# A gated delta rule in chunks of 128 tokens instead of 64, in a fused attention and MLP block on one Trainium2 core

## The reference

```python
h = rms_norm(x, pre_mix_norm)
proj = h @ w_in                     # q, k, v, gates of both mixers
fox_o = forgetting_attention(...)   # 8 heads x 64, causal, softmax
# gated delta rule, 4 heads x 128, chunk = C tokens
decay = exp(gc[:, None] - gc[None, :])          # lower triangle
m     = strict_lower((k * beta) @ k.T) * decay
t_inv = inverse(I + m)
u, w  = t_inv @ (v * beta), t_inv @ (k * beta * exp(gc))
a     = (q @ k.T) * decay
for each chunk:
    v_new = u - w @ state
    o     = (q * exp(gc)) @ state + a @ v_new
    state = state * exp(gc[-1]) + (k * exp(gc[-1] - gc)).T @ v_new
x = x + rms_norm(concat(fox_o, gdn_o) @ w_out)
x = x + rms_norm(relu(rms_norm(x) @ w_up) ** 2 @ w_down)
```

## Time and profile before

| | |
|---|---|
| median of three runs | 1646.76 us (1643.49 to 1648.24) |
| the profiled execution's own time | 1642.12 us |
| its span in the profile | 1640.1 us |
| PE busy | 1534.6 us, 94% |
| DVE, ACT, POOL busy | 56%, 40%, 36% |

### The profile page before, as it was taken

How to read it: one execution, slowest core, us unless ns; L and a number is a source line. 1 busy time by engine, 2 the same in 40 slices (tenths; PEclk the granted TensorE clock), 3 DMA queues, 4 the chain that set the end, 5 groups by cost and what they waited for, 6 DMA issues and landing times.

```text
span 1640.1 us, 22146 instructions
## 1 busy us (share of the span) xinstructions
PE 1534.6 (94%) x7769; PEld 1231.6 (75%) x7769; DVE 924.5 (56%) x1538; ACT 652.0 (40%) x1371; POOL 585.0 (36%) x496
## 2 busy tenths in 40 slices
PE   4999999999999999998987998999999999899997
PEld 3877876787777877787765886788787786688885
DVE  5355256542565335645342459776676659944557
ACT  4343245522445234453441435233332343345444
POOL 1005133341324322252330026666665429831001
PEclk7999999999999999999677998999999999999999
DMA  5111001200102011011104333444444696333533
GB/s 186 39 58 34 14 21 32 66 26 14 52 7 59 27 27 39 14 52 52 40 1 165 117 103 96 142 141 148 143 152 143 215 375 209 85 97 98 196 97 140
DMA packets 135043, 152.75 MB, mean 93 GB/s; under 512 B 9436, under 2 KB 89612, under 8 KB 134936
## 3 DMA queue, kind: packets, MB, share of 16 engines
q1 hardware_dynamic: 134936, 151.32, 28.6%
HBM read 109.31 MB, written 41.99 MB: 92 GB/s over the span
## 4 chain that ended last, share of the span: by engine, by line
PE 67%; DVE 13%; POOL 6%; issue 6%; DMA 5%; ACT 2%; SPq 0%; DVEq 0%; POOLq 0%; ACTq 0%
PE ps L2085 7%; PE ps L2028 6%; PE ps L2029 6%; PE ps L2030 6%; PE ps L2333 4%; PE ps L2335 4%; PE ps L2334 4%; PE ps L2187 4%; PE ps L2320 3%; PE ps L2321 3%; PE ps L2322 3%; DVE db_lo L1755 3%; DVE da_lo L1753 3%; DMA w_bot<-in_w_up_dram 3%; PE ps L2273 2%
## 5 line engine op out<-in xcount | busy, mean ns | idle before, releaser
L2028 PE MATMUL ps<-big_hi,w_hi 128*128 128x512 f32 x464 | 213.8, 461 | 0.0
L2333 PE MATMUL ps<-db_hi,da_hi 128*128 128x512 f32 x448 | 177.6, 396 | 11.3 <-DVE db_lo L1755 11.3
L2029 PE MATMUL ps<-big_lo,w_hi 128*128 128x512 f32 x464 | 186.2, 401 | 0.0
L2030 PE MATMUL ps<-big_hi,w_lo 128*128 128x512 f32 x464 | 184.9, 399 | 0.0
L2334 PE MATMUL ps<-db_lo,da_hi 128*128 128x512 f32 x448 | 174.5, 390 | 0.0
L2335 PE MATMUL ps<-db_hi,da_lo 128*128 128x512 f32 x448 | 174.5, 390 | 0.0
L1753 DVE TENSOR_TENSOR da_lo<-a_raw,da_hi 128x512 fp32r<-128x512 f32 x112 | 103.4, 923 | 101.0 <-ACT da_hi L1302 100.9
L1302 ACT ACTIVATE da_hi<-a_raw 128x512 fp32r<-128x512 f32 x112 | 70.7, 631 | 173.8 <-PE ps L2335 151.1
L2320 PE MATMUL ps<-bt_hi,ring_hi 128*128 128x512 f32 x320 | 127.5, 398 | 4.3 <-DVE ring_lo L1675 3.6
L2322 PE MATMUL ps<-bt_hi,ring_lo 128*128 128x512 f32 x320 | 128.1, 400 | 0.0
L2321 PE MATMUL ps<-bt_lo,ring_hi 128*128 128x512 f32 x320 | 127.7, 399 | 0.0
(11 more groups left out here) (283 smaller groups left out, 3473.0 us busy)
## 6 DMA issues: line engine op xcount, KB each, us to landing
a_raw<-act_dram SPq DMA_DIRECT2D x112, 256.0 KB, 2.6
act_dram<-s_act SPq DMA_DIRECT2D x64, 256.0 KB, 2.0
wd<-in_w_down_dram SPq DMA_DIRECT2D x15, 1024.0 KB, 7.1
w_raw<-in_w_in_dram SPq DMA_DIRECT2D x28, 512.0 KB, 3.9
act_dram<-c SPq DMA_DIRECT2D x48, 256.0 KB, 5.0
w_raw<-in_w_up_dram SPq DMA_DIRECT2D x18, 512.0 KB, 4.5
w_bot<-in_w_up_dram SPq DMA_DIRECT2D x16, 512.0 KB, 5.7
x_in<-in_x_dram SPq DMA_DIRECT2D x8, 512.0 KB, 6.5
```

What stands on the lines that cost most here:

```text
L2028: nc.tensor.matmul(acc, w_hi[s][:, k, :], rhs_hi, start=(k == 0), stop=False)
L2029: nc.tensor.matmul(acc, w_hi[s][:, k, :], rhs_lo, start=False, stop=False)
L2030: last = nc.tensor.matmul(acc, w_lo[s][:, k, :], rhs_hi, start=False, stop=(k == KT - 1))
L2333: nc.tensor.matmul(acc, da_hi[s][:, cols], db_hi[s][:, :], start=start, stop=False, skip_group_check=True)
```

## The change

The chunk is 128 tokens. The scan does one chunk for every two attention tiles, in the even steps only, with full 128x128 products. The inverse has a seventh level. So `PREP_FILLS` has six more fills (`TX`, `XR` of level 5 and `X` of level 6 for each half, in other words: `TX 5`, `X 6`, `XR 6` twice). The mask of the last level lies in a tile of its own, two scratch tiles of ScalarE become parts of `kn` and `qn`, and the number of steps of the stage is now written `NFT` (16), since `NCHUNK` is 8. The contents of the constant inputs (masks, `keep`) follow the chunk. The core of the diff:

```diff
-CHUNK = 64
+CHUNK = 128
-LEVELS = 6
+LEVELS = 7
...
-    ("TX", 1, 3), ("XR", 1, 3), ("XR", 0, 5), ("X", 1, 4), ("W", 0, 0), ("U", 0, 0),
-    ("TX", 1, 4), ("XR", 1, 4), ("X", 1, 5), ("XR", 1, 5), ("W", 1, 0), ("U", 1, 0),
+    ("TX", 1, 3), ("XR", 1, 3), ("TX", 0, 5), ("XR", 0, 5), ("X", 1, 4), ("X", 0, 6),
+    ("TX", 1, 4), ("XR", 1, 4), ("XR", 0, 6), ("X", 1, 5), ("W", 0, 0), ("U", 0, 0),
+    ("TX", 1, 5), ("XR", 1, 5), ("X", 1, 6), ("XR", 1, 6), ("W", 1, 0), ("U", 1, 0),
...
+        last_level = held(mix, "last_level", [P, P])
-        sq_scratch = held(mix, "sq_scratch", [P, FOX_DIM])
-        sq_scratch2 = held(mix, "sq_scratch2", [P, GDN_DIM])
+        sq_scratch, sq_scratch2 = kn[:, 0, 0:FOX_DIM], qn[:, 0, :]
...
# ScalarE
-                        rows, (g, tt) = slice(64 * (i % 2), 64 * (i % 2) + 64), divmod(i // 2, 4)
-                        act.wait_ge(scan_o, j * NCHUNK + i + 1)
-                        nc.scalar.activation(xb[rows, g, tt, :], scan_b[rows, 0:P], ACT.Copy).then_inc(o_read, 1)
+                        if i % 2 == 0:
+                            g, tt = divmod(i // 2, 4)
+                            act.wait_ge(scan_o, j * NCHUNK + i // 2 + 1)
+                            nc.scalar.activation(xb[:, g, tt, :], scan_b[:, 0:P], ACT.Copy).then_inc(o_read, 1)
# VectorE
-                        rows, (g, tt) = slice(64 * (i % 2), 64 * (i % 2) + 64), divmod(i // 2, 4)
-                        dve.wait_ge(scan_v, j * NCHUNK + i + 1)
-                        nc.vector.tensor_tensor(v_new[rows, :], xb[rows, g, tt, :], scan_a[rows, 0:P], ALU.subtract).then_inc(v_new_ready, 1)
+                        if i % 2 == 0:
+                            g, tt = divmod(i // 2, 4)
+                            dve.wait_ge(scan_v, j * NCHUNK + i // 2 + 1)
+                            nc.vector.tensor_tensor(v_new[:, :], xb[:, g, tt, :], scan_a[:, 0:P], ALU.subtract).then_inc(v_new_ready, 1)
...
-                        dve.wait_ge(scan_s, j * NCHUNK + i + 1)
+                        if i % 2 == 0:
+                            dve.wait_ge(scan_s, j * NCHUNK + i // 2 + 1)
# TensorE
-                        nc.tensor.matmul(scan_a[rows, 0:P], t_inv[:, g, tt, toks], state[:, :], start=True, stop=True).then_inc(scan_v, 1)
-                        nc.tensor.matmul(scan_b[rows, 0:P], qdT[:, i // 2, toks], state[:, :], start=True, stop=False)
+                        if step:
+                            nc.tensor.matmul(scan_a[:, 0:P], t_inv[:, g, tt, :], state[:, :], start=True, stop=True).then_inc(scan_v, 1)
+                            nc.tensor.matmul(scan_b[:, 0:P], qdT[:, c, :], state[:, :], start=True, stop=False)
...
-                    if i < NCHUNK:
-                        nc.tensor.matmul(scan_a[:, P:2 * P], kd[rows, i // 2, :], v_new[rows, :], start=True, stop=True).then_inc(scan_s, 1)
-                        nc.tensor.matmul(scan_b[rows, 0:P], a_t[rows, i // 2, toks], v_new[rows, :], start=False, stop=True).then_inc(scan_o, 1)
+                    if step:
+                        nc.tensor.matmul(scan_a[:, P:2 * P], kd[:, c, :], v_new[:, :], start=True, stop=True).then_inc(scan_s, 1)
+                        nc.tensor.matmul(scan_b[:, 0:P], a_t[:, c, :], v_new[:, :], start=False, stop=True).then_inc(scan_o, 1)
```

More of the change, by code:

```diff
@@ L254, in build @@
         whole = ctx.enter_context(ExitStack())
[L255 removed]
+        const = held(whole, "const", [P, N_CONST - 1, P])
         big = ctx.enter_context(ExitStack())
@@ L1111, in gdn_square @@
                         act.wait_ge(tail_square, j * (NFT + NT) + 3 * t - 1)
-                    act.wait_ge(o_read, j * NCHUNK + 2 * t + 2)
-                    nc.scalar.activation(sq_scratch2[:, :], xb[:, g, tt, :], ACT.Square,
+                    act.wait_ge(o_read, j * NCHUNK + t + 1)
+                    nc.scalar.activation(sq_scratch2, xb[:, g, tt, :], ACT.Square,
                                          accum_out=tail_ss[:, tail_gdn(g) + tt:tail_gdn(g) + tt + 1]).then_inc(tail_square, 1)
                 copy_queries(0)
-                for i in range(NCHUNK + 1):
-                    if i + 1 < NCHUNK:
+                for i in range(NFT + 1):
+                    if i + 1 < NFT:
                         copy_queries(i + 1)
@@ L2191, in beside_scan @@
                 def beside_scan(i, n):
-                    if with_gemm and i < NCHUNK:
+                    if with_gemm and i < NFT:
                         unit_index, k = divmod(SCAN_STEP_PARTS * i + n, KT)
                         part(SCAN_UNITS[unit_index], j + 1, k)
[L2197 to L2202, removed]
-                        nc.tensor.matmul(scan_a[rows, 0:P], t_inv[:, g, tt, toks], state[:, :], start=True, stop=True).then_inc(scan_v, 1)
-                        if i >= 2:
-                            pe.wait_ge(o_read, j * NCHUNK + i - 1)
-                        nc.tensor.matmul(scan_b[rows, 0:P], qdT[:, i // 2, toks], state[:, :], start=True, stop=False)
+                for i in range(NFT + 1):
+                    c = i // 2
+                    step = i % 2 == 0 and c < NCHUNK
+                    if i < NFT:
+                        if step:
+                            g, tt = divmod(c, 4)
+                            pe.wait_ge(state_ready, j * (NCHUNK + 1) + c + 1)
+                            nc.tensor.matmul(scan_a[:, 0:P], t_inv[:, g, tt, :], state[:, :], start=True, stop=True).then_inc(scan_v, 1)
+                            if c >= 1:
+                                pe.wait_ge(o_read, j * NCHUNK + c)
+                            nc.tensor.matmul(scan_b[:, 0:P], qdT[:, c, :], state[:, :], start=True, stop=False)
                         hh, qb = FOX_TILES[i]
@@ L2214, in head @@
                         nk = (qb + 1) * P
[L2215 to L2219, removed]
+                        for ks in range(0, nk, 512):
+                            ke = min(ks + 512, nk)
+                            nc.tensor.matmul(fox_s[:, ks:ke], q_hi[i % 2][:, :], k_split[hh][:, ks:ke], start=True, stop=False)
+                            nc.tensor.matmul(fox_s[:, ks:ke], q_lo[i % 2][:, :], k_split[hh][:, ks:ke], start=False, stop=True)
                         nc.tensor.matmul(fox_s[:, qb * P:nk], ident_bf[:, :], causal_bf[:, :], start=False, stop=True,
```

21 lines of the change are left out of this document (11 added, 10 removed).

## The result

The changed kernel takes 1599.32 us (median of 4, 1599.18 to 1601.09) against 1645.7 (median of 4) for the kernel before on the same chip: ratio 0.972, 95% interval 0.971 to 0.974, 46 us faster. The forecast was 1630 with a range from 1616 to 1645. The direction was right; the gain was nearly three times the one forecast, and lies outside the range.

The account below looks back on a forecast made before the run. PE's instruction issue was taken to bound heads 0 to 2, and in head 3 also PE's waits. Scans -31.5 and -8.6, preparation +23.6, sum -16.5 us: from 1646.8 to 1630, range 1616 to 1645.

Parts of the forecast that it names:

- The preparation: Preparation, all heads: six added fills a head, 21.6 us, plus 2.0 of uncovered waits; +23.6 us, bounds 21.4 and 26.
- bare ends: End of the preparation, heads 0 to 2: waits for copies left uncovered, 0.27 and 0.4 us; 2.0 us over three heads.
- The odd steps, heads 0 to 2: Scan, heads 0 to 2: without its delta-rule products an odd step saves 1.54 us, 12.3 us a head.
- The even steps: Scan: products with wider weights add 0.15 us a step, 1.2 us a head; between nothing and 0.3 a step.
- step 7: Scan step 7: DVE's order makes the copy of turned blocks late for PE, costing 0.6 us a head.
- Head 3: Scan of head 3, which has no part there: -8.6 us, bounds 4 and 12.
- my first rival: Odd steps of the scan: attention's chain over three engines takes back what PE saves; 1661 us, chance 0.10.
- my third rival: Scan of head 3: a less busy PE has five more steps at 1.2 GHz; 8 us, 1638; chance 0.12.
- More than I count: Scan and preparation: even steps free, copies covered, the preparation's ends covered; 1621 us, chance 0.12.
- The weight loads in full: Scan: loads cost 0.3 us a step instead of 0.15, copies late in half the odd steps; 1640 us, chance 0.12.
- My sign of being wrong: Scan: PE waits for `probs_t` copies or the maximum in odd steps, 0.3 us first matmuls, or head 3's clock under 0.7.
- head 3 at its best: Scan of head 3: the larger bound of its saving, 12 us, used for the low end of the range.

Follow-up runs that it names:

- the split runs: Changed kernel with the first, the first two, or all four products of each step as two matmuls of 64 columns: 1604.84, 1606.28 and 1610.98 us.

## Why the prediction was wrong

**The preparation: right.** +23.6 forecast, +24.0 in the stages of the run with the preparation alone, +26.3 in the changed kernel. The ends were 1.81 and 2.01 where I had 1.86 and 1.95, and head 0, which nothing else disturbed, rose by 6.0 (99.1 against 93.1), which is 6 x 0.89 and 0.64 of bare ends. What came on top in heads 1 and 2 is a longer pause at the head's start, where no release is named (2.6 and 2.8 us against 1.7 and 2.2), and the clock. At the first half's third level, where no part is placed, PE waits for DVE:

```profile
341.53 3.14 PE L2090 MATMUL ps<-t_inv,n_lev 128*128 128x128 f32 x16 [1.85 <-DVE t_inv L1535]
344.32 0.77 PE L2033 MATMUL ps<-big_hi,w_hi 128*128 128x512 f32 x1
```

The kernel before has the same wait at the same place:

```profile
349.35 2.05 PE L2085 MATMUL ps<-t_inv,n_lev 128*128 128x128 f32 x16 [1.85 <-DVE t_inv L1532]
351.15 0.48 PE L2028 MATMUL ps<-big_hi,w_hi 128*128 128x512 f32 x1
```

So the wait of 1.85 us is not the seventh level's. What differs is what follows it: in heads 1 and 2 of the changed kernel PE then ran at 1.2 GHz for a while (granted clock 0.50 from 343.0 to 345.7, the matmul 0.77 in place of 0.48), and from the start behind the wait to the next fill it took 4.19 us in place of 2.59, 1.6 us a time. The clock fell there in none of the heads before, in head 2 alone in the run with the preparation alone, in heads 1 and 2 of the full products with the old preparation, and in heads 0 and 2 of the changed kernel's repeat. A drop comes or doesn't come behind the same wait; it belongs to neither version of the preparation, and such drops are part of the spread between executions.

**The odd steps, heads 0 to 2: the pitch was right, its reading wrong.** I took 1.54 us from an odd step. A pair of steps fell from 10.42 to 8.09 us in head 1 (from w@state of step 2 to that of step 4, 407.02 to 417.44 before and 403.05 to 411.15 after), by 2.33: that is 1.54 and the 0.81 of the even step. But once all products are full, removing the odd step's is worth only 0.75 to 0.89 us (8.16 against 7.27 in the table above, and 9.13 against 8.38 for the next two steps). About half of the 1.54 was never the products' own time; it was the changes of size around them, which sixteen steps of full products save as well.

**The even steps: the step that failed.** "Products with 128 columns of weights in place of 64 ... three products of two matmuls each are six loads, between nothing ... and 0.3 us." I priced the difference by the loads and set its lower bound at nothing, though the earlier trace rows held the comparison: the first pair took 0.91 us, where a stream of full products at the 0.11 a matmul that I used beside it gives 4 x 0.11 and the part's own 0.23, 0.67. I used both numbers and never asked why four smaller matmuls should take longer than four full ones. The term was +1.2 us a head and should have been -8 x 0.81 = -6.5. With it the sum for heads 0 to 2 is 12.3 + 6.5 - 0.6 = 18.2 a head, where 16.3 was measured. Most of the 1.9 is waits that the faster PE met, beyond the 0.6 that I had for step 7: in head 1's scan 1.3 us for copies of turned blocks, where there were none, and 1.6 for v_new, where there were 1.1.

The rule of the Trainium skill that I weighed, that a weight load grows with its columns, agrees with the earlier trace rows (six times its 48 ns is 0.29 us a step, not the 0.32 that I wrote) and decides nothing here: the products with the longer loads took the shorter time, and two of them in a row start 0.22 us apart (411.15 and 411.37), which is the 0.11 a matmul of the stream in which I had taken the loads as hidden. The rule that bears on the case I had overlooked: "TensorEngine Tiling (Array Packing)", section "Key Properties", says that a change of the tiling mode drains TensorE, and a change to another tile of the same mode does not. The runs agree with both halves as far as time goes: 0.14 to 0.20 us a change, and no such step between the two halves of a split product, which start 0.01 us apart. That the time is spent on a drain is the page's word; no row here shows one.

**Head 3: -8.6 forecast, -19.8 measured.** The stages divide it: full size alone took it from 88.7 to 72.7 us (-16.0), and from the run with full products and seven levels (72.8) to the changed kernel (68.9) the odd steps gave 3.9, 0.5 us each. In the repeats on one chip they gave less still (70.2 and 68.7), so neither figure is firm. That is my first rival, in head 3 above all: PE waits for the copies of the turned blocks. The waits of PE in head 3's scan after:

```profile
PE ps L2183 <- ACT probs_t L1089: 4.4, 7, 1.2
PE ps L2192 <- DVE probs_t L1551: 4.1, 5, 1.2
PE ps L2192 <- ACT probs_t L1089: 2.3, 4, 0.7
PE ps L2209 <- DVE state L1574: 2.2, 1, 2.2
PE ps L2224 <- POOL q_lo L1893: 1.6, 3, 0.7
```

The first three, 10.8 us, are for these copies; they were 3.7 before and 5.8 with full products and the old chunk. The clock went the other way than my third rival had it: 0.72 over the scan before, 0.88 with full products and the old chunk, 0.83 after; by the same formula as there 51, 17 and 23 us of the scan were at 1.2 GHz. PE was busy 83.7 of 90.6 us before, and 62.0 of 72.7 with full products. At full clock the size alone is worth 16 x 0.81 = 13 of the 16 us. How much of the rest the clock gave, and why it was granted more with full products, isn't settled: the split runs had clocks of 0.75 to 0.81 in no order of their half-size products.

**The rivals and the range.** "More than I count" had the sign of the miss and 1621 us, but its lowest term for an even step was nothing. The weight loads in full did not appear. My sign of being wrong, waits of PE for copies of `probs_t`, did come in heads 0 to 2, with one of 0.9 us, but small beside the gain. The range reached down to 1616 by even steps that cost nothing extra, bare ends covered and head 3 at its best. No term of it let an even step become cheaper, so no combination of them could reach 1599.

## What to carry to other kernels

Read the tile size that the rows print beside each matmul. Where a small product stands among full ones, compare its start-to-start time with that of a full product before pricing it by its size: here each change of tile cost about 0.16 us, more than the 0.11 of a full matmul, and filling the array with zeros was worth 45 us of 1642. If a product must be small, put those of one tile size next to each other, and its halves side by side. When a change removes and enlarges work at once, price the enlarged work alone first; a run that does only that would have shown that the new chunk size gains nothing by itself.

## What the runs showed of the hardware that I had not expected

- A change between tile sizes of TensorE costs 0.14 to 0.20 us at full clock, whether columns or rows are cut; at such a place no wait is named, and PE's busy share stays high (94% before).
- The two 64-column halves of a product run side by side: four matmuls in 0.27 us, where two full ones took 0.22.
- Moving one product out of a pair, with the same matmuls, cost 22 us.
- Behind the same wait of 1.85 us the granted clock fell to 1.2 GHz in some heads and executions and not in others; each drop there cost 1.6 us.
- A lone float32 product of full size between full ones costs 0.23 us of PE's time, one of 64 columns 0.57. This is read to the second matmul behind it (417.19 - 416.50 and 429.39 - 428.36, less 2 x 0.23), since the first one behind it starts early and its successor late.
